# Where the low parts of the weights stand at stage ends and in the first chunks, a first down piece in bank order, and later turning steps in the second mixer

## The reference

```python
def first_block(x, ...):
    for layer in range(2):
        x = x + 0.5 * swiglu(rmsnorm(x, ffn1_norm[layer]), ffn1_w_gu[layer], ffn1_w_down[layer])
        h = rmsnorm(x, mix_norm[layer])
        if layer % 2 == 0:
            y = mixer_gated_deltanet(h, ...)            # stage mixer_a
        else:
            y = mixer_sliding_window_sinks(h, ...)      # stage mixer_b
        x = x + y
        x = x + 0.5 * swiglu(rmsnorm(x, ffn2_norm[layer]), ffn2_w_gu[layer], ffn2_w_down[layer])
    return rmsnorm(x, final_norm)

def second_block(x, p, ...):
    h = rms_norm(x, norm_mix)
    ...                                                 # stage hybrid: attention and RWKV beside each other
    x = x + merged @ w_out
    x = x + jnp.square(jax.nn.relu(rms_norm(x, norm_ffn) @ w_ff1)) @ w_ff2      # stage ffn4
    return x + (p @ w_ple) * jax.nn.sigmoid(rms_norm(x, norm_ple) @ w_ple_gate)  # stage ple
```

## Time and profile before

| | us |
|---|---|
| median of 3 runs | 1714.46 |
| lowest, highest | 1705.96, 1714.79 |
| the profiled execution | 1712.38 |
| its span, clock granted on average | 1710.2, 0.968 |
| PE busy in it | 1592.5 |

### The profile page before, as it was taken

The page is one execution under the profiler, slowest core; times in us unless marked ns, Lnnn a source line. Parts: engine busy times, 40 slices in busy tenths (PEclk is TensorE's granted clock), DMA queues, the critical chain, the costliest instruction groups (busy, mean ns, idle before and its releaser), DMA issues.

```text
span 1710.2 us, 35864 instructions
## 1 busy us (share of the span) xinstructions
PE 1592.5 (93%) x15411; PEld 1528.2 (89%) x15411; DVE 1055.4 (62%) x1274; ACT 728.0 (43%) x811; POOL 67.4 (4%) x53
## 2 busy tenths in 40 slices
PE   7999999878899999999898999999969999899997
PEld 6999899777899999999888999999957778899997
DVE  4765577653666556764576665568666654776445
ACT  4443345532443344343455443464543322455333
POOL 1000000000100001000101000021110000100000
PEclk9999999989999999999899999999989998999999
DMA  8665545001566555655333665554200021455551
GB/s 280 199 196 177 189 131 169 26 2 39 172 195 194 188 173 177 193 196 192 128 100 124 197 196 181 189 175 140 74 2 2 2 101 51 159 181 177 189 190 41
DMA packets 155063, 243.23 MB, mean 142 GB/s; under 512 B 9283, under 2 KB 106174, under 8 KB 154814
## 3 DMA queue, kind: packets, MB, share of 16 engines
q1 hardware_dynamic: 154510, 240.63, 43.4%
q10 hardware_dynamic: 432, 0.79, 0.2%
HBM read 240.34 MB, written 1.05 MB: 141 GB/s over the span
## 4 chain that ended last, share of the span: by engine, by line
PE 81%; DVE 10%; ACT 5%; issue 2%; DMA 0%; POOL 0%; SPq 0%; DVEq 0%; ACTq 0%
PE dense_ps L2388 22%; PE dense_ps L2389 21%; PE dense_ps L2390 21%; PE mixer_ps L456 3%; DVE w_lo L2757 3%; ACT w_hi L2590 2%; PE dense_ps L456 2%; PE mixer_ps L1082 1%; PE mixer_ps L1655 1%; DVE qkv L887 1%; PE mixer_ps L1100 1%; PE mixer_ps L1091 1%; ACT ly_r L502 0%; PE mixer_ps L1661 0%; DVE h_lo L2824 0%
## 5 line engine op out<-in xcount | busy, mean ns | idle before, releaser
L2757 DVE TENSOR_TENSOR w_lo<-raw,w_hi 128x2048 fp32r<-128x2048 f32 x223 | 511.8, 2295 | 419.3 <-ACT w_hi L2590 418.5
L2388 PE MATMUL dense_ps<-h_hi,w_hi 128*128 128x256 f32 x2368 | 669.9, 283 | 29.0 <-DVE h_lo L2824 16.0
L2389 PE MATMUL dense_ps<-h_lo,w_hi 128*128 128x256 f32 x2368 | 662.2, 280 | 0.0
L2390 PE MATMUL dense_ps<-h_hi,w_lo 128*128 128x256 f32 x2368 | 661.9, 280 | 0.0
L2590 ACT ACTIVATE w_hi<-raw 128x2048 fp32r<-128x2048 f32 x223 | 427.7, 1918 | 505.1 <-PE dense_ps L2390 487.4
L2388 PEld LDWEIGHTS dense_ps<-h_hi,w_hi 128*128 128x128 f32 x2368 | 451.2, 191 | 37.4 <-issue 27.7
L2389 PEld LDWEIGHTS dense_ps<-h_lo,w_hi 128*128 128x128 f32 x2368 | 451.3, 191 | 0.8 <-issue 0.5
L2390 PEld LDWEIGHTS dense_ps<-h_hi,w_lo 128*128 128x128 f32 x2368 | 451.8, 191 | 0.0
L2388 PE MATMUL dense_ps<-g_hi,w_hi 128*128 128x256 f32 x960 | 267.4, 279 | 7.6 <-DVE full L2915 5.5
L2389 PE MATMUL dense_ps<-g_lo,w_hi 128*128 128x256 f32 x960 | 266.7, 278 | 0.0
L2390 PE MATMUL dense_ps<-g_hi,w_lo 128*128 128x256 f32 x960 | 266.7, 278 | 0.0
(11 more groups left out here) (526 smaller groups left out, 1845.9 us busy)
## 6 DMA issues: line engine op xcount, KB each, us to landing
raw<-in_ffn_w_gu SPq DMA_DIRECT2D x176, 512.0 KB, 4.7
raw<-in_ffn_w_down SPq DMA_DIRECT2D x88, 512.0 KB, 4.2
raw<-in_w_ff SPq DMA_DIRECT2D x64, 512.0 KB, 4.3
raw<-in_w_in SPq DMA_DIRECT2D x36, 512.0 KB, 4.4
raw<-in_a_w_in SPq DMA_DIRECT2D x32, 512.0 KB, 4.4
raw<-in_a_w_out SPq DMA_DIRECT2D x8, 512.0 KB, 4.3
raw<-in_b_w_in SPq DMA_DIRECT2D x8, 512.0 KB, 4.2
raw<-in_b_w_out SPq DMA_DIRECT2D x8, 512.0 KB, 4.2
```

Of the source, the lines that this page charges most:

```text
L2388: pe.matmul(o, hi, mh, start=start, stop=False)
L2389: pe.matmul(o, hi, ml, start=False, stop=False)
L2390: return pe.matmul(o, lo, mh, start=False, stop=stop)
L2757: dve.tensor_tensor(w_lo[:, p % 2, :], raw[:, p % RAW_SLOTS, :], w_hi[:, p % 2, :].bitcast(F32), ALU.subtract).then_inc(lo_ready, 1)
```

## The change

1. *Bank pairs*: `halves=True` for the down job of all five ffn stages: the first piece goes pair by pair, and starts when the first pair is drained.
2. *Second chunk's split*: in the ffn stages, ACT and DVE split the fourth piece (second of chunk 1) before the norm's scale is waited for, no longer behind it; the loops over chunks run from the second chunk on (`lead`), four passes in place of five. In mixer_b ACT moves it ahead of the masks, DVE moves it from ahead of the first drain to behind the bias.
3. *Residual ahead of the low part*: at the end of every stage but ffn0, DVE adds the first pair into `xT` before it makes the low part of the next stage's first piece; this low part then stands ahead of `h_lo`. mixer_a, mixer_b, hybrid and the step from ffn4 to ple are in it.
4. *Turning steps*: beside b_out, PE has a callback each quarter piece. `scores` and `values` stay where they were; `turned_` of the group before now comes a quarter piece behind them.
5. The norm sums of hybrid move from behind the second to behind the fourth of eight steps of chunk 1.

```diff
@@ mixer_b, PE
-        def beside_output(k):
-            if k == 0:
-                pe.wait_ge(b_qkv, 3)
-                scores(4)
-                turned_(3)
-            if 1 <= k <= 5:
-                values(k + 2)
-            if 1 <= k <= 3:
-                scores(k + 4)
-            if 1 <= k <= 4:
-                turned_(k + 3)
+        def beside_output(at_):
+            half, mid = at_ // 2, at_ % 2 == 0
+            if half > 5:
+                return
+            if mid:
+                if half:
+                    turned_(half + 2)
+                return
+            if half:
+                values(half + 2)
+            if half < 4:
+                if half == 0:
+                    pe.wait_ge(b_qkv, 3)
+                scores(half + 4)
@@ mixer_b, DVE
-        splits(1)
         drained(0)
         biased(0)
+        splits(1)
         keys_kept(0)
...
         kept(7)
-        splits(1)
         f0 = FILL_OF["b_out"]
...
-            if e:
-                splits(1)
+            splits(1)
@@ hybrid, PE
-            if (c, kt) == (1, 1):
+            if (c, kt) == (1, 3):
                 norms()
@@ ffn stages, PE
-                    wide(down, g_hi, g_lo, (g_ready, lambda r: chunk_of[up] + r + 1))
+                    wide(down, g_hi, g_lo, (g_ready, lambda r: chunk_of[up] + r + 1), halves=True)
@@ narrow of DVE (ACT's has the same)
                 if stage_of[job] in SPLIT_AHEAD:
+                    lead = int(stage_of[job] in LATE_SCALE and first == 0)
+                    if lead:
+                        dve.wait_ge(piece_used, p0 + 2)
+                        body(0, 0)
+                        split_lo(0, 0)
+                        ahead[0] += 1
@@ norm of ACT and of DVE
-                    splits(1)
+                    splits(1 if stage in ("mixer_b", "hybrid") else 2)
@@ residual of DVE, for all jobs but down0
+                    if e == 0 and ahead_of_split:
+                        splits(1)
```

More of the change, by code:

```diff
@@ L1240, in beside_input @@
                 values(2)
-        def beside_output(k):
-            if k == 0:
-                pe.wait_ge(b_qkv, 3)
-                scores(4)
-                turned_(3)
-            if 1 <= k <= 5:
-                values(k + 2)
-            if 1 <= k <= 3:
-                scores(k + 4)
-            if 1 <= k <= 4:
-                turned_(k + 3)
+        def beside_output(at_):
[12 more added lines that the diff above has]
+                scores(half + 4)
         run_narrow("b_in", beside_input)
-        wide("b_out", ao_hi_b, ao_lo_b, (att_out, lambda r: 2 * r + 2), beside=beside_output, halves=True)
+        wide("b_out", ao_hi_b, ao_lo_b, (att_out, lambda r: 2 * r + 2), quarter=beside_output, halves=True)
     def mixer_b_act(act, link, narrow, splits):
         weights, turned_kept = att_act_steps(act, groups_b, small_b, buf_b, 0, places_c())
+        splits(1)
         att_masks_kept(act, masks_b)
-        splits(2)
+        splits(1)
         weights(0)
@@ L2214, in hybrid_dve @@
                 splits(1)
-        splits(3)
+        splits(2)
     def ple_act(act, link, splits):
@@ L2440, in run_narrow, with wide @@
                     chunk(c, 0)
-            def wide(job, mh, ml, ready=None, beside=lambda k: None, midway=lambda: None, halves=False):
+            def wide(job, mh, ml, ready=None, beside=lambda k: None, midway=lambda: None, halves=False,
+                     quarter=lambda at_: None):
                 p0, f0, n = PIECE_OF[job], FILL_OF[job], COUNT_OF[job]
@@ L2470, in wide @@
                             last.then_inc(half_filled, 1)
+                        if not final and at_ % 4 == 3:
+                            quarter(4 * r + at_ // 4)
                         if not final and at_ == 7:
@@ L2776, in narrow @@
                 if stage_of[job] in SPLIT_AHEAD:
-                    def turn(t):
-                        for q in range(2):
-                            split_lo(t, 2 * q)
-                            dve.wait_ge(piece_used, p0 + 2 * q + 2 + 4 * t)
-                            body(2 * t + q, q)
-                            split_lo(t, 2 * q + 1)
-                    turns = (n - 1) // 2 if close else n // 2
+                    lead = int(stage_of[job] in LATE_SCALE and first == 0)
+                    if lead:
+                        dve.wait_ge(piece_used, p0 + 2)
+                        body(0, 0)
+                        split_lo(0, 0)
+                        ahead[0] += 1
+                    def turn(t):
+                        for i in range(2):
+                            c = lead + i
+                            split_lo(t, 2 * i)
+                            dve.wait_ge(piece_used, p0 + 2 * c + 2 + 4 * t)
+                            body(2 * t + c, c % 2)
+                            split_lo(t, 2 * i + 1)
+                    turns = (n - lead - 1) // 2 if close else (n - lead) // 2
                     repeat(dve, turns, turn, link, 2 * links)
                     ahead[0] += 4 * turns
-                    for c in range(2 * turns, n):
+                    for c in range(lead + 2 * turns, n):
                         closing = close and c == n - 1
@@ L2856, in next_stage, with residual @@
                 return STAGES[STAGES.index(s) + 1]
-            def residual(job, scale):
+            def residual(job, scale, ahead_of_split=False):
                 f0 = FILL_OF[job]
@@ L2937, in _ @@
                     else:
-                        splits(pieces_of[down] - 1)
-                    residual(down, 1.0 if up == "ff1" else 0.5)
+                        splits(pieces_of[down] - 2)
+                    residual(down, 1.0 if up == "ff1" else 0.5, s != "ffn0")
                 elif s == "mixer_a":
                     mixer_a_dve(dve, link, narrow, splits, split_act)
-                    residual("a_out", 1.0)
+                    residual("a_out", 1.0, True)
                 elif s == "mixer_b":
@@ L2946, in _ @@
                     hybrid_dve(dve, link, narrow, splits, split_act, by_rms)
-                    residual("out2", 1.0)
+                    residual("out2", 1.0, True)
                 elif s == "ple":
```

20 lines of the change are left out of this document (12 added, 8 removed).

## The result

The changed kernel takes 1695.34 us (median of seven runs, 1687.57 to 1699.18) against 1714.46 before (seven runs, 1705.96 to 1716.87): a ratio of 0.9885, 95% interval 0.9859 to 0.9911. In a second set of runs it was 1689.93 against 1710.00, again 0.9885 (0.9856 to 0.9913). The prediction was 1693.0, with 1685 to 1703 as its range.

A forecast was written before the change was run, and what follows sets the result against it. PE, busy 1592.5 of 1710.2 us, sets the end, so only its waits or low-clock time can be won. Terms sum to 20.1 us off 1712.4, giving 1692.3; 0.7 added makes 1693, range 1685 to 1703.

The forecast's parts named there:

- bank pairs, ffn0 to ffn3: First down piece: drain waits of 1.54 us go, 0.15 to 0.25 returns at the second piece; 5.2 us won.
- end of mixer_b, ple: Low part moved behind the residual makes PE wait longer: 1.1 us lost at mixer_b's end, 0.9 at ple.
- start of mixer_b with its clock: Turning of the keys: PE's wait goes, 4.5 us won, plus 1.9 from half clock behind it.
- turning steps / their clock: Beside b_out: shorter waits before `turned_` win 0.8 us, and half a stretch worth 1.6 another 0.8.
- norm sums, with hybrid's stretch: Hybrid, chunk 2: later sums make the low part late, 1.5 us lost; the stretch at its start going wins 1.7.
- so a piece takes PE 5.65 us: Pace of PE's pieces, read from ACT's piece starts in a wide job and used throughout the forecast.
- All of it comes back: 0: Bank pairs in ffn4: the drain wait saved returns at the second down piece, whose low part does not move; gain 0.
- The clock: Half-clock stretches behind PE's pauses at stage ends, mixer_b's start and b_out mostly vanish: 6.0 us won, between 1 and 9.
- rival 1: Whole kernel: the low clock stays, only 16.0 us arrive, 1696.4 us, or 1700 with other stretches falling worse; 20%.
- 2: ffn0 to ffn3: the next wait takes over as in ffn4, 10.2 us of gains vanish, 1702.5 us; 8%.
- 3: Chunk loop becomes DVE's, so slower: with 1.2 us added per chunk, 1723 us; 3%.
- 4: mixer_b gains nothing, as the earlier keys meet the next wait in the attention chain: 1698.7 us; 9%.

The follow-up runs named there:

- dve_sums: Changed kernel with mixer_b-end and ple low parts back ahead of the residual, hybrid norm sums back at chunk 1 step 1, VectorE adding second norm's squares: 1689.21 us, ratio 0.9872.
- before_again: The kernel before, executed once more unaltered: 1717.97 us.
- norm_back: Changed kernel with hybrid's norm sums back at chunk 1, step 1: 1695.39 us, ratio 0.9915 to before.
- all_back: Changed kernel with hybrid's norm sums back and low part again ahead of residual at ends of mixer_b and ffn4: 1693.07 us, ratio 0.9899 to before.

## Why the prediction was right, and where it was not

| term | forecast | measured, pace loss off |
|---|---|---|
| second chunk's split, ffn0 to ffn3 / ffn4 | 5.0 / 0.1 | pauses of 5.4 less four times 0.11: 5.0 / 0.1 |
| bank pairs, ffn0 to ffn3 | 5.2 | about 3.7 (fast pace) to 5.4 (slow) |
| bank pairs, ffn4 | 0 | -2.0 |
| residual first, five stage ends | 2.0 | 2.4 |
| end of mixer_b, ple | -1.1, -0.9 | -1.2, -1.1 |
| start of mixer_b with its clock | 6.4 | 6.4 |
| turning steps / their clock | 0.8 / 0.8 | 0.4 / 1.5 |
| norm sums, with hybrid's stretch | -1.5 + 1.7 | -0.1 |
| stage ends' stretches (other two) | 2.5 | 2.9 (1.45 each) in the first execution |

**Mechanisms.** Nearly every wait that the prediction names went or came at its place, and the clock went the way it says at every place but ffn4. The time agrees with the sum of 20.1: 21.3 us at equal pace, and 19.1 and 20.1 between the medians. How near it came is luck in part. The measured column adds up to 18.0 to 19.7, and at least 3.3 of the 23.0 us between the first two executions belong to no term: 1.4 in hybrid behind its input projections and 0.8 in ffn0 apart from its waits; the rest was not traced.

**The step that went wrong: "so a piece takes PE 5.65 us"**. It took that for the kernel's pace; it is the pace of that stretch of that execution. 28% of the dense matmuls before ran at it, 44% after. This is no term of the change, so it moves the sum of a profiled pair by several us (here -7.6) and the ratio of the medians hardly (0.9885 both times). It did bend one term, the bank pairs: at 5.44 us a piece PE arrives 0.2 us earlier per piece, and the wait at the second down piece is 0.42 and not 0.15 to 0.25.

**The term that was missed: bank pairs in ffn4.** "All of it comes back: 0" counted idle time alone. Two pauses of 1.46 and 1.18 us joined into one of 2.65, and the longer one had a stretch behind it: of ten executions with the pairs nine have a stretch there (`dve_sums` has none), of the four without the pairs none has. The prediction weighed the clock at every other pause, and not at the one that the change made longer.

**The clock.** Forecast 6.0. In the first execution 4.4 came at the stage ends, 1.9 at mixer_b's start (if the rest of that term is as forecast) and 1.5 at b_out, and 1.5 or more was lost in ff2: at most 6.3, close for partly the wrong reasons. A stretch cost 1.4 to 1.5 us of stage length behind ffn1, where the prediction took 1.7; all three stage ends lost theirs, where it counted on 2.5; and b_out gave back a whole stretch where it took half. That the turning steps came out near 1.6 is luck: their waits were worth half the forecast and their clock twice. Against `before_again`, which has two stretches at stage ends, it is 1.5 less. The end of mixer_b, which the prediction called an even chance, had a stretch in one of four executions with the pause of 2.39. The Trainium skill ("TensorE: Matmul & The Clock Gate", Part 1) calls the phase at a kernel's start run-variable, which no single execution could show. The two executions of before agree, and in mid-kernel too: behind the same pause of 2.38 us at hybrid's end the first has a stretch and the second none.

**Norm sums.** The price was right and the reading of it was not. "Where the old place had 0.6 us to spare" holds only while chunk 0 is slowed by a stretch. I took GpSimd's durations from that one execution, and gave no thought to what its additions do beside VectorE.

**Rivals.** 1 did not come true: in both executions of after no stage end from 430 to 1500 us has a stretch. The time alone could not have told it from the sum: the profiled execution took 1697.04 us, and rival 1 said 1696.4. 2, 3 and 4 are each refuted by a run of its part alone.

## What to carry to other kernels

When a pause is shortened, ask what the clock did behind it, and when two pauses merge, ask the same: the idle time may be unchanged and the total still worse. Before a step is moved, look at what the other engines do at the new time; the additions on GpSimd here lasted over three times as long when VectorE's subtraction had begun. When a term comes out as forecast, check its parts too: the turning steps did, with both parts off by a factor of two. And compare two profiled executions only after counting matmuls in a window without waits: here one kernel differs from itself by more than most single edits are worth.

## What the runs showed of the hardware that I had not expected

**TensorE streams at two paces under the same granted clock of 1.00.** Steps of 113, 113 and 114 ns repeat at the fast one, of 117 to 119 at the slow one. A pace holds for a whole stage of a hundred us and changes almost only where PE has waited or taken in a short step of another kind, if only for 0.2 us, or where the clock changed. Neither the line nor the length of the pause fixes which comes: behind the same pause of 1.95 us, ahead of gu2, the first execution of after went slow and the second fast. In 14 executions 12% to 67% of the dense matmuls were slow, a pace loss of 6 to 32 us. The two ends are `norm_back` (1684.05 us in its profiled execution) and `all_back` (1702.16). What picks the pace is open; no run was made for it.

**GpSimd's addition of 128x256 elements lasted 0.73 to 0.81 us or 2.65 to 2.75**, nothing between, by whether VectorE's two-input subtraction had begun. It goes the other way as well: 76 of these subtractions began while an addition was under way, and they lasted up to 3.09 us where one alone takes 2.29. In the changed kernel the long addition stands at the start of ffn1, ffn2, mixer_b, ffn3 and ffn4 too, where the sums are wanted later: in the first execution PE waits at them for 0.1 us at most, in the second once for 0.3, in ffn3.
